# A hybrid transformer layer pair on one core: the first norm by halves, turned tiles copied by VectorE, and matmuls reordered in two attention-like stages

## The reference

```python
# first block
h = rms_norm(x, norm_mix_pre)
c_q, c_kv, k_rope, sc_b, sc_c, sc_h, ssd_in = split(h @ w_in)
y = concat(mla_mixer(c_q, c_kv, k_rope), short_conv_mixer(sc_b, sc_c, sc_h), ssd_mixer(ssd_in))
x = x + rms_norm(y @ w_out, norm_mix_post)
u = causal_dwconv(rms_norm(x, norm_ffn_pre) @ ffn_w_up) + ffn_conv_b
gate, up = split(u)
x = x + rms_norm((silu(gate) * up) @ ffn_w_down, norm_ffn_post)
# second block
h = rms_norm(x, norm_pre_2)
qa, ka, va, za, qb, kb, vb, ob, zb, ig, fg, ga, gb = split(h @ w_in_2)
ya = rms_norm(diff_attention(qa, ka, va, lam)) * silu(za)
yb = rms_norm(sigmoid(ob) * mlstm(silu(conv(qb)), silu(conv(kb)), vb, ig + b_i, fg + b_f)) * silu(zb)
merged = sigmoid(ga) * (ya @ w_a) + sigmoid(gb) * (yb @ w_b)
x = x + rms_norm(merged @ w_out_2, norm_post_2)
```

## Time and profile before

| | us |
|---|---|
| median of 3 runs | 2355.34 |
| the profiled execution, its own time | 2356.65 |
| its span | 2354.8 |
| TensorE matmuls busy | 2241.4 (95%) |
| VectorE busy | 1171.3 (50%) |
| GpSimd busy | 1019.8 (43%) |
| ScalarE busy | 716.1 (30%) |

### The profile page before, as it was taken

How to read it: one execution, slowest core, us unless ns; L and a number is a source line. 1 busy time by engine, 2 the same in 40 slices (tenths; PEclk the granted TensorE clock), 3 DMA queues, 4 the chain that set the end, 5 groups by cost and what they waited for, 6 DMA issues and landing times.

```text
span 2354.8 us, 27395 instructions
## 1 busy us (share of the span) xinstructions
PE 2241.4 (95%) x9862; PEld 1737.9 (74%) x9862; DVE 1171.3 (50%) x1239; ACT 716.1 (30%) x1131; POOL 1019.8 (43%) x821
## 2 busy tenths in 40 slices
PE   6999999889899999999999987999999998999998
PEld 5777755567688888888887766777767776788877
DVE  5864355536663333333334787666665455411123
ACT  4343255533311111111112343555344333200112
POOL 2533410167554444444444662222244552444475
PEclk8999999999999999999999998999999999999999
DMA  5111100032211111111111230000101111111143
GB/s 196 54 36 36 36 10 10 10 134 81 63 54 53 45 53 45 45 53 45 53 45 45 76 142 28 28 27 27 36 28 45 45 40 32 45 45 47 51 161 116
DMA packets 34031, 130.61 MB, mean 55 GB/s; under 512 B 4132, under 2 KB 4516, under 8 KB 33196
## 3 DMA queue, kind: packets, MB, share of 16 engines
q1 hardware_dynamic: 30960, 111.39, 14.7%
q10 hardware_dynamic: 3004, 18.30, 2.1%
HBM read 117.04 MB, written 12.58 MB: 55 GB/s over the span
## 4 chain that ended last, share of the span: by engine, by line
PE 82%; DVE 9%; ACT 4%; issue 3%; DMA 1%; POOL 1%; SPq 0%; DVEq 0%; ACTq 0%; POOLq 0%
PE PG L666 13%; PE PG L672 13%; PE PG L671 13%; PE PG L1192 5%; PE PG L1198 5%; PE PG L1197 5%; PE PG L1013 2%; PE PO L1040 1%; PE PO L1263 1%; PE PT L1027 1%; PE PG L719 1%; PE PG L724 1%; PE PG L725 1%; DMA WR<-weights 1%; PE PO L764 1%
## 5 line engine op out<-in xcount | busy, mean ns | idle before, releaser
L559 POOL TENSOR_TENSOR WH<-WR,zero 128x512 fp32r<-128x512 f32 x380 | 418.1, 1100 | 1230.0 <-PE PG L666 679.6
L562 POOL TENSOR_TENSOR WL<-WR,WH 128x512 fp32r<-128x512 f32 x380 | 540.0, 1421 | 29.8
L666 PE MATMUL PG<-HH,WH 128*128 128x512 f32 x1136 | 449.2, 395 | 3.2 <-issue 2.3
L672 PE MATMUL PG<-HH,WL 128*128 128x512 f32 x1136 | 443.0, 390 | 0.0
L671 PE MATMUL PG<-HL,WH 128*128 128x512 f32 x1136 | 442.6, 390 | 0.0
L666 PEld LDWEIGHTS PG<-HH,WH 128*128 128x128 f32 x1136 | 213.7, 188 | 52.4 <-issue 6.2
L671 PEld LDWEIGHTS PG<-HL,WH 128*128 128x128 f32 x1136 | 213.8, 188 | 46.1 <-issue 2.2
L672 PEld LDWEIGHTS PG<-HH,WL 128*128 128x128 f32 x1136 | 213.6, 188 | 44.8
L1192 PE MATMUL PG<-HH,WH 128*128 128x512 f32 x544 | 229.1, 421 | 5.4 <-ACTq L2025 2.7
L1198 PE MATMUL PG<-HH,WL 128*128 128x512 f32 x544 | 214.6, 394 | 0.0
L1197 PE MATMUL PG<-HL,WH 128*128 128x512 f32 x544 | 214.1, 394 | 0.0
(11 more groups left out here) (535 smaller groups left out, 4147.8 us busy)
## 6 DMA issues: line engine op xcount, KB each, us to landing
WR<-weights SPq DMA_DIRECT2D x196, 512.0 KB, 3.5
RAW<-x SPq DMA_DIRECT2D x8, 512.0 KB, 8.0
x_spill<-X ACTq DMA_DIRECT2D x1, 4096.0 KB, 12.8
X<-x_spill ACTq DMA_DIRECT2D x1, 4096.0 KB, 12.1
x_spill<-X ACTq DMA_DIRECT2D x4, 1024.0 KB, 5.4
X<-x_spill ACTq DMA_DIRECT2D x8, 512.0 KB, 3.9
y<-RAW SPq DMA_DIRECT2D x7, 512.0 KB, 5.1
POSI<-positions ACTq DMA_DIRECT2D x1, 512.0 KB, 15.4
```

Of the source, the lines that this page charges most:

```text
L559: pool.tensor_tensor(WH[:, slot, part], WR[:, slot, part], zero[:, :].to_broadcast([P, HALF]), ALU.add).then_inc(w_hi, 1)
L562: pool.tensor_tensor(WL[:, slot, part], WR[:, slot, part], WH[:, slot, part].bitcast(F32), ALU.subtract).then_inc(w_split, 1)
L666: m = pe.matmul(out[:, cut], WH[:, slot, w], hi[:, cut], start=n == 0, stop=False)
L672: m = pe.matmul(out[:, cut], WL[:, slot, w], hi[:, cut], start=False, stop=last)
```

## The change

The diff, cut to its core (small parts that only follow from these are left out; semaphores are renumbered with them):

```diff
-NORMS = [("mix_pre", 1), ("q", 2), ("kv", 1), ("ssd", 2)]
+NORMS = [("mix_pre", 2), ("q", 2), ("kv", 1), ("ssd", 2)]
+ACT_TURNED = 4
...
-            norm("mix_pre")
+            for h in range(2):
+                pe.wait_ge(n_sq, h + 1)
+                pe.matmul(PO[:, h, :], ones, SQ[:, 0, halves(h)], start=True, stop=True).then_inc(n_sq_used, 1)
...
+                def early_values(j):
+                    if j == 0:
+                        pe.wait_ge(t_free, i * 24 + 8)
                         primed(pe, att_free, i)
                         pe.wait_ge(n_done, NDONE["ssd"])
+                    value(0, j).then_inc(pv_half, 1)
+                def late_values():
+                    pe.wait_ge(t_free, i * 24 + 24)
+                    for j in range(TT):
+                        m = value(1, j)
+                    m.then_inc(pv_half, 1)
...
                     if t == 4:
-                        values(0)
+                        early_values(0)
+                    transposes(t, 0)
+                    if 4 <= t < 7:
+                        early_values(t - 3)
+                    transposes(t, 1)
+                if i < 3:
+                    pe.wait_ge(krot_done, 2 * i + 4)
                     for hh in range(2):
-                        transposes(t, hh)
-                values(1)
+                        scores(0, hh, i + 1)
+                late_values()
...
-            pe.wait_ge(aug_k, 1)
             with pe.Fori(0, DIFF_HEADS - 1) as i:
...
                     if last:
-                        next_head(max(j - 4, 0), max(j - 3, 0))
+                        next_head(*{0: (0, 2), 2: (2, 3), 3: (3, 4)}.get(j, (0, 0)))
...
+                if last:
+                    return
                 pe.wait_ge(m_sq, i + 1)
-                spread(hb, 4 if last else 12, ones, SQ[:, 0, :])
+                spread(hb, 12, ones, SQ[:, 0, :])
...
+            def last_norm():
+                pe.wait_ge(m_sq, ML_HEADS)
+                for m in (4, 5):
+                    hb.before(pe, m)
+                    pe.matmul(PT[:, m % 2, :], ones, SQ[:, 0, halves(m)], start=True, stop=True)
+            projection("merge", g, 0, 2, HH, HL, early=last_norm)
             primed(pe, m_pp, ML_HEADS * TT)
+            projection("merge", g, 1, 3, HH, HL)
...
-            wait_split("y")
             def mixers(g, k, u, i=0, stride=0):
                 for n in range(2):
                     slot = unit("merge", u, i, stride, n)
+                    pe.wait_ge(s_lo, SPLIT0["y"] + 4 * n + 4)
...
             act.wait_ge(consts_ready, 1)
+            act.activation(cols[:, 15:16], v("eps"), ACT.Sqrt)
...
-                if t % 2 == 0:
+                if t == ACT_TURNED:
                     g.ready(act, t)
...
-                primed(act, pv_half, 4 * i + 4)
+                if i < 3:
+                    exp(0, 0, i + 1)
+                    exp(0, 1, i + 1)
+                primed(act, pv_half, 5 * i + 5)
                 act.activation(RAW[:, i, :], POf, ACT.Copy).then_inc(att_free, 1)
...
-            log1p_rows(1, flat, 2)
-            wide = Wide(DIFF_WIDE)
-            wide.ready(act, 0)
-            act.activation(NK[:, :], wide.psum(0), ACT.Copy).then_inc(wide.free(0), 1)
             g.wait_free(act, 1)
...
             queries_high(QHL, d_qhi)
+            act.wait_ge(aug_k, 1)
+            act.wait_ge(lam_loaded, 80)
+            for rows, c in ((slice(64, 66), 0), (slice(0, 2), 1)):
+                act.activation(QHA[rows, c, :], AUG[rows, 0, :], ACT.Copy)
+                act.activation(KLA[rows, c, :], AUG[rows, 1, :], ACT.Copy, scale=0.25)
+            wide = Wide(DIFF_WIDE)
+            wide.ready(act, 0)
+            act.activation(NK[:, :], wide.psum(0), ACT.Copy).then_inc(wide.free(0), 1)
             keys_high()
...
-            act.wait_ge(aug_k, 1)
             queries_high(QHA, d_qb)
+            log1p_rows(1, flat, 2)
+            g.ready(act, 2)
+            act.activation(RAW[:, 0, :], g.psum(2), ACT.Silu).then_inc(g.free(2), 1)
             act.wait_ge(forget_made, 1)
             for at in (0, 4):
                 act.dma_start(GROWS[2][at:at + 4, :], flat[0]).then_inc(forget_back, 16)
-            g.ready(act, 2)
-            act.activation(RAW[:, 0, :], g.psum(2), ACT.Silu).then_inc(g.free(2), 1)
...
                     if last and j == 6:
                         merge_gate(0)
+                        merge_gate(1)
...
                 if last:
                     merge_gate(2)
+                    merge_gate(3)
...
-            for t in range(1, TT, 2):
+            for t in [t for t in range(TT) if t != ACT_TURNED]:
                 g.ready(dve, t)
                 dve.tensor_copy(X[:, :, t * P:(t + 1) * P],
...
-            factors("mix_pre", cols[:, 0:TT], SQ[:, 0, :]).then_inc(n_sq, 1)
+            root_reciprocal("mix_pre", cols[:, 0:TT])
+            for h in range(2):
+                factors(cols[:, 4 * h:4 * h + 4], SQ[:, 0, halves(h)], 4).then_inc(n_sq, 1)
...
-            for rows, c in ((slice(64, 66), 0), (slice(0, 2), 1)):
-                step(dve.tensor_copy(QHA[rows, c, :], AUG[rows, 0, :]))
-                step(dve.tensor_scalar(KLA[rows, c, :], AUG[rows, 1, :], 0.25, None, ALU.mult))
...
-            def first_operands():
-                queries_low(0)
-                keys_low(0)
+            queries_low(0)
+            keys_low(0)
...
-            softplus(flat, None, None, 3, first_operands)
+            softplus(flat, None, None, 3)
```

More of the change, by code:

```diff
@@ L677, in unit, with projection, second @@
                 return unit_slot(stage, k)
-            def projection(stage, g, k, u, hi, lo, i=0, stride=0, between=lambda: None):
+            def projection(stage, g, k, u, hi, lo, i=0, stride=0, between=lambda: None, early=lambda: None):
+                def second():
+                    unit(stage, u, i, stride, 1)
+                    early()
                 slot = unit(stage, u, i, stride)
@@ L682, in projection @@
                 product(g.psum(k), [(slot, b, hi[:, b, :], lo[:, b, :]) for b in range(KT)],
-                        w_used[1], (1, KT // 2), lambda: unit(stage, u, i, stride, 1), between).then_inc(g_ready, 1)
+                        w_used[1], (1, KT // 2), second, between).then_inc(g_ready, 1)
             def first_pair(stage, g, k, name, hi=HH, lo=HL):
@@ L1006, in _, with scores @@
             for i in range(MLA_HEADS // 2):
-                def scores(t, hh):
+                def scores(t, hh, i=i):
                     n = mla_group(i, t, hh)
@@ L1412, in _ @@
             mlstm_head(ML_HEADS - 1, True)
+            hb = Halves("mlstm", ML_HEADS - 1, ML_HALVES)
+            for m in (2, 3):
+                hb.wait_free(pe, m)
+            g = Groups("merge_first")
+            def last_norm():
+                pe.wait_ge(m_sq, ML_HEADS)
+                for m in (4, 5):
+                    hb.before(pe, m)
+                    pe.matmul(PT[:, m % 2, :], ones, SQ[:, 0, halves(m)], start=True, stop=True)                      .then_inc(hb_ready, 1)
+            projection("merge", g, 0, 2, HH, HL, early=last_norm)
             primed(pe, m_pp, ML_HEADS * TT)
+            projection("merge", g, 1, 3, HH, HL)
             for m in (4, 5):
-                Halves("mlstm", ML_HEADS - 1, ML_HALVES).wait_free(pe, m)
-            g = Groups("merge_first")
-            for k in range(2):
-                projection("merge", g, k, 2 + k, HH, HL)
-            wait_split("y")
+                hb.wait_free(pe, m)
             def mixers(g, k, u, i=0, stride=0):
@@ L2137, in mlstm_head @@
                             next_half(m)
-                if last:
-                    merge_gate(1)
-                else:
+                if not last:
                     act.wait_ge(m_scores, i * TT + TT)
@@ L2163, in mlstm_head @@
                 act.activation(SQ[:, 0, :], MH[:, :], ACT.Square).then_inc(m_sq, 1)
-                if last:
-                    merge_gate(3)
-                else:
+                if not last:
                     for m in (10, 11):
@@ L2175, in mlstm_head @@
                     hb.ready(act, m)
-                    act.activation(RS[:, halves(m)], hb.bank(m), ACT.Sqrt, bias=v("eps"),
+                    act.activation(RS[:, halves(m)], PT[:, m % 2, :] if last else hb.bank(m), ACT.Sqrt, bias=v("eps"),
                                    scale=1.0 / P).then_inc(m_root, 1)
@@ L2357, in _, with softplus @@
             norm_split("mix_pre", "norm_mix_pre", lambda k: X[:, k, :], HL)
-            def softplus(rows, raw, bias, n_act, between=None):
+            def softplus(rows, raw, bias, n_act):
                 x0, y, u, l, s = rows[0:5]
@@ L2373, in softplus @@
                 step(dve.tensor_tensor(s, s, y, ALU.mult))
-                if between is not None:
-                    between()
                 dve.wait_ge(rows_act, n_act + 2)
@@ L2614, in _ @@
             short_conv(1)
[L2615 removed]
```

(2 more changed lines are left out.)

65 lines of the change are left out of this document (35 added, 30 removed).

## The result

The changed kernel takes **2317.81 us**, median of 4 runs (2314.98 to 2321.19), against 2356.43 for the kernel before (4 runs, 2355.04 to 2357.83): ratio 0.9837, 95% interval 0.9820 to 0.9854. Forecast were 2318.4 (2309 to 2329) and faster. The profiled execution took 2318.93, its span is 2317.1, 37.7 less than before.

The account below looks back on a forecast made before the run. TensorE, busy 2241.4 of 2354.8 us, was taken as the bound, losing by idling and lower clock. Terms 6.3 + 11.5 + 6.5 + 12.6 = 36.9 took the profiled 2356.65 to 2319.8, median 2318.4, range 2309 to 2329.

Parts of the forecast that it names:

- Front, 6.3: Front, up to the first projection tiles: shorter chain and less half clock win 6.3 us, between 3.7 and 8.2.
- one drop of medium length: Front: the clock, with two gaps left, was assumed to fall once for a medium time, giving 6.3 us.
- the lower end, 3.7: Front: only 3.7 us won if the clock stays down as long as in the kernel before.
- the first rival: Clock and hidden chains hold: front 3.7, second block 3, pieces 8, last head 9; 23.7 us won, 2331.6; chance 0.17.
- Attention, 11.5: Attention: pieces of values in gaps 5.6, scores ahead at pair turns 4.8, clock 1.1; 11.5 us won.
- Second block's start, 6.5: Start of the second block: first scores 5.7 us earlier, second scores at 1420.4 instead of 1426.97; 6.5 us won.
- Last head, 12.6: Last head and merge: idle 12.9 plus clock 3.4, less new waits 3.7; 12.6 us won.
- the bare steps: Last head, j = 4 to 7: nothing covers scores, decay, values; fits but for 0.2 us.
- the second rival: More falls away: front's clock stays up, dips in first differential head go; 44.5 us won, 2310.8; chance 0.13.
- The attention at half clock: Slower rival: small pieces and transposes make TensorE run two of four attention pairs at 1.2 GHz; 2402 us; chance 0.01.
- tied to an old wait: Rival, attention: PT's slots or banks tie the pieces to old waits; attention brings 5, total 2325; chance 0.07.
- the one table load: Front, rival case: if the first table does not serve the squares, a load of 1.28 us comes back.

Follow-up runs that it names:

- e5: The changed kernel itself, unaltered, measured and profiled once more: 2320.03 us (2315.80 to 2323.61).
- e9: The changed kernel with the next pair's first scores and exponentials back behind the late products, early pieces of the values kept: 2321.63 us.
- e2: The changed kernel with the attention as before, without early pieces of the values or scores ahead of the late products: 2332.06 us.
- e8: The changed kernel with ScalarE's Sigmoid table loaded before YH and the merge's first gate made after YH's third tile: 2321.03 us.

## Why the prediction was right, and where it was not

- **Front, 6.3.** In the pair of profiles 5.5, over eleven profiles 3.2: the term is about twice too large. The step that failed is the choice between the ends, "I take one drop of medium length". Of the 6.3, 2.6 stood for clock that comes back. It did not: both new gaps (2.15 and 3.47 against the forecast 2.5 and 3.3) let the clock fall, and behind the norm's first matmul the new front is only 0.5 faster than the old. In seven of the nine profiles it is down without a break from the norm's matmuls well into the first pair. So the lower end, 3.7, was the likely value; the first rival had it. The Trainium skill, page "TensorE: Matmul & The Clock Gate", section "HAM oscillation — how this bites in real kernels", describes short bursts of matmuls between waits that each start at the lower clock, and the traces agree with it: 0.50 in 22 to 34 us in e5. The rest of the step came as written, shifted by the arrival of x: one table load, one wait of ScalarE at tile 4 (1.13, forecast 1.8), root before VectorE's last copy, projection at 27.49 (but at 29.66 in e5, past the 26 to 29 that were to show the prediction right). The diagonals were too low, 1.07 to 1.6 a half for 0.87.
- **Attention, 11.5.** Measured 11.6: pieces 1.21 a pair for 1.39, turns 1.62 for 1.6, clock 1.8 for 1.1. e9 took the turns away, and its profile found 4.9 plus the drop; its median shows 2.7 to 3.8 of these 6.7. The half clock at the third turn, of which I had counted 1.1, came back in both profiles that have the old turns (e2, e9) and is absent from all that have the new.
- **Second block's start, 6.5.** Measured 8.9; right mechanism, wrong size. In the time of before, VectorE's key parts end at 1406.9, not 1408.7 (3.60 for 4.17, and ScalarE's copies follow each other up to 0.1 closer than their 1.05); the softplus ends at 1414.8, not 1417.3; the Silu, forecast behind its load to 1415.1, now waits 0.54 for TensorE's group and ends at 1413.7. So the first scores come at 1414.25, and the second at 1418.0 for 1420.4. The position rows, of which I had no duration, took 1.04, the upper bound that I had taken.
- **Last head, 12.6.** Measured 12.5. New waits: bank 0.30 for 0.85, `ME` 0.53 for 0.4, Sigmoid 0.73 for 0.6, `mixers` 2.49 for 1.7, none in the bare steps: 4.05 for 3.7.
- **What stood in no term.** The two drops inside the first differential head went (2.8), which I had given only to the second rival. Against it 2.0 and 1.6 were lost to drops in stretches that nobody touched. Together these come to -0.8. That the total is right to a microsecond is luck: a term too small by 2.4 and one too large by 0.8 in this profile, by 3 on average, offset each other. 3.2 + 11.6 + 8.9 + 12.5 is 36.2, and the sum was 36.9. The runs of one kernel alone spread over more than that.
- **Rivals.** The attention at half clock did not come; no piece was tied to an old wait (at t = 4 the wait is gone, and 0.26 and 0.39 are left at t = 5 and 6); the one table load serves the squares and the root.

## What to carry to other kernels

Give the clock its own line in the sum, for each gap that stays, and take the price of the drop in full unless the gap is gone: splitting a gap of 5.6 us, with 3.8 behind it, into 2.2 and 3.5 did not save the clock. Where a wait of a chain of other engines can't be filled with work, matmuls into a bank that the next product starts anew kept the clock up behind every wait that they filled. They must stand exactly in the wait, since outside they cost up to their full time. And they pay only where TensorE sets the pace behind the wait: 2.6 us before the output projection, nothing in the two prologues, where VectorE does. And before a difference of 1 to 3 us between two profiles is given a cause, profile the same kernel twice.

## What the runs showed of the hardware that was not expected

Whether the clock falls behind a given short gap is not fixed by the program: the drop behind the wait of 1.82 is in the first profile of the change and not in e5, of the same program. Over all 14 profiles, in which these stretches have the same order, the wait of 1.82 had a drop behind it in 8 and the wait of 2.67 at 1267 us in 9, the waits of 6.30 each time that they were left unfilled. The Trainium skill, same page, section "What's actually happening", says that the chip looks at TensorE's activity on a rhythm of its own, not tied to the kernel, so that the same kernel measures differently from run to run. The traces agree: the nine runs of the change took 2315 to 2324 us, the slower the lower their mean granted clock (0.993 to 0.989). That spread is larger than most single steps here. Filling five waits took most of the drops out of one execution, also at short waits that were not filled; why those stayed up is not explained, and was not tried further.

VectorE's time for one and the same instruction depends on what GpSimd does beside it. Of YL's eight tiles (128 x 1024), those with no GpSimd work beside them, or with `WH<-WR,zero` alone, take 1.21 to 1.23 us. Those that share time with `WL<-WR,WH` take 2.06 to 2.32, but for one of 1.30 that had begun 0.3 us ahead of it. There are three such tiles in the change, four in e8 and five in the kernel before, which gives the 11.9, 13.1 and 13.2 us of the eight. A kernel without the split beside them was not run, so this is read from the times of the traces alone. GpSimd works beside the spread diagonals in every profile too, and their first half takes 0.7 to 1.5 us, their second 1.5 or 1.75.
